# Small parameters loaded first, input-projection units 4 and 5 ahead of 6 and 7, products of 32 and 64 rows grouped, and new orders in both mixing stages of a two-layer hybrid encoder

## The chip, the cores and the metric

The kernel runs on one core of a Trainium2 chip. The metric is the device time in microseconds (us) of one execution. TensorE is PE in the rows (PEld is its weight load), VectorE is DVE, ScalarE is ACT, GpSimd is POOL and SyncE is SP. Every number is float32.

## What is computed

Two layers over 256 tokens of width 1024. Each layer has a token mixer of four head groups of 256 columns (retention, S5, Hyena, mLSTM) between one input and one output projection, then a channel mixer: dense SwiGLU in layer 0, the two best of eight experts in layer 1.

```python
h = layer_norm(x, ln_in_w, ln_in_b)
for l in range(DEPTH):                                  # DEPTH = 2
    proj = h @ w_in[l]                                  # 256 x 1024 @ 1024 x 3088
    y = concatenate([retention_mixer(p_ret, ...), s5_mixer(p_s5, ...),
                     hyena_mixer(p_hy, ...), mlstm_mixer(p_ml, ...)])
    h = layer_norm(DN_ALPHA * h + y @ w_out[l], ln1_w[l], ln1_b[l])
    f = swiglu(h, ...) if l % 2 == 0 else moe_swiglu(h, ...)
    h = layer_norm(DN_ALPHA * h + f, ln2_w[l], ln2_b[l])

# hyena_filters: a filter generator, one per layer
h = sin(fr * (z @ w1 + b1)); h = sin(fr * (h @ w2 + b2)); h = (h @ w3).reshape(L, 2, 2, D_GROUP)
h = h * exp(-t * rates)
return h * rsqrt(sum(square(h), axis=(0, 2)))
```

S5 is a diagonal complex recurrence, forward and backward in time. Hyena multiplies spectra twice: its value goes to frequencies, is multiplied by the filter's spectrum and comes back, and this is done for each of two filters. Retention and mLSTM are chunked attentions with decays, each followed by a norm over heads.

## The kernel before, in words

**How it is ordered.** No compiler orders the work. Each engine runs a list of calls written out by hand (`mix_0` and `mix_1` exist once for TensorE, once for ScalarE and once for VectorE), and the engines meet in named semaphores. An engine never passes a call that waits. So the place of a call in its list decides what is queued behind its wait.

**The input projection.** It is cut into 12 units. Units 0 to 5 give transposed outputs of 256 columns each (0 is the S5 input, 1 to 3 are Hyena's three parts, 4 and 5 are mLSTM's query and key), in two halves of eight products each, `unit(l, i, 0)` and `unit(l, i, 1)`. Units 6 and 7 are the retention's query and key for the two token tiles, 8 and 9 its value and gate, 10 and 11 mLSTM's value and gate. `UNITS` is the order, `UNIT_BANK` the PSUM bank of each, and `WIN_LOADS` says which units share one of the 2 MB weight loads into the three buffers `win0` to `win2`. Before a unit writes to its bank, the unit that had the bank must have been taken out: by `conv` on VectorE for units 1 to 5 (after ScalarE's `take_unit`), by `rotary` for 6 and 7, by `take_unit` for the others.

**S5.** Eight tiles. `s5_in` multiplies 32 rows of the input (K = 32) into a bank. VectorE then does for each tile `s5_tile_products`, `s5_tile_scan` and `s5_tile_rotate`, and GpSimd adds two halves (`b_sum`). `s5_y` gathers four tiles, `s5_skip` and `s5_glu` end it. The tables of sines that the tiles need come from steps `pre(l, 13)` to `pre(l, 20)`: VectorE reduces an angle, ScalarE takes sine and cosine. `s5_angle`, `pre(l, 11)` and `pre(l, 12)` prepare the coefficients.

**Hyena's filters.** Steps `pre(l, 0)` and `pre(l, 1)` are the two sine layers, `pre(l, 2)` to `pre(l, 5)` the third product with K = 64, window and square, `pre(l, 6)` the norm (a sum of squares by a product with ones, which two-column outputs take), `pre(l, 7)` to `pre(l, 10)` the filter's spectrum. In layer 0 these steps run inside `mix_0`, in layer 1 inside the dense channel mixer. `pre_norm` is VectorE's reciprocal of the norm.

**The rest of a mixing stage.** `hyena_transposes`, `hyena_forward`, `hyena_product` (VectorE), `hyena_inverse` and `hyena_gate` (VectorE), twice; `ret_transposes`, `ret_scores`, `ret_decay`, `ret_out` and `ret_norm`; `ml_gate_rows`, `ml_rows_a`, `ml_log`, `ml_rows_b`, `ml_columns`, `ml_cols`; `ml_rows_out` and `ml_rows_back` store the row maxima to memory and read them back spread over all partitions, both issued by ScalarE, the second after the first has landed; then for four heads `ml_mask`, `ml_exps`, `ml_weights`, `ml_out`, and last `ml_norm`, `head_scale(1)`, `head_out(1)`. The output projection is cut into 16 `out_product` calls, which fill TensorE's time between these; six of them stand behind `head_out(1)`.

**Loads.** SyncE issues all of them in one list. At the start: x, the first norm's weights, the identity, the first unit weights, all parameters of layer 0 (`pr`, 1728 KB), the positions and other small constants, and so on. A buffer of unit weights is loaded again when the last unit that reads it has been computed.

Of the kernel before, what the change touches and what calls it, by code (L numbers as in the profile page):

```python
# [19 lines left out]
P = 128  # L20
D = 1024
L = 256
# [45 lines left out]
def columns(sizes):  # L68
# [15 lines left out]
    ("s5_c", 2 * 16 * 32), ("s5_b", 512), ("glu", 512), ("hy_w3", 1024), ("hy_w12", 64), ("gate_w", KT * 16),  # L84
# [4 lines left out]
def trunk(nc, x, ln, const, par, w_in, w_out, ffn, moe, tab, out):  # L89
    ctx = ExitStack()  # L90
    with ctx:
# [82 lines left out]
        w1_feat = pr[64:97, PAR["hy_w12"][0]:PAR["hy_w12"][1]]  # L174
# [46 lines left out]
        fx_ = [[a[0:64, i * 256:(i + 1) * 256] for i in range(4)] for a in work]  # L221
# [3 lines left out]
        ct_s = [yTf[:, i * 512:(i + 1) * 512].rearrange("p (j c) -> p j c", c=32) for i in range(4)]  # L225
# [39 lines left out]
        s_pos = sem("positions_in")  # L265
        win_in = [sem(f"win{i}_loaded") for i in range(3)]
        loaded = [sem(f"ffn_slot{i}_loaded") for i in range(SLOTS)]
        freed = sem("ffn_chunk_split")
        up_in = [sem(f"ex_up_loaded{i}") for i in range(SLOTS)]
# [73 lines left out]

        def win_use(l, j):
# [18 lines left out]

        PRE1 = {u: k for u, k in enumerate(tuple(range(11, 21)) + tuple(range(7)), start=2)}
# [8 lines left out]
        def _(sp):  # L373
            def load_ff(i):
                s, _ = ff_use(i)
                if i >= 3:
                    sp.wait_ge(freed, i - 2)
                sp.dma_start(ring[s][:, :], ffn[i]).then_inc(loaded[s], 16)

            def load_win(l, j):  # L380
                b, _ = win_use(l, j)
                if j >= 3:
                    before = WIN_LOADS[{3: 1, 4: 2, 5: 0}[j]] if j < 6 else WIN_LOADS[j - 3]
# [16 lines left out]
            def load_ln(n):  # L400
                if n == 2:
                    sp.wait_ge(f_pm, 2)
                    sp.wait_ge(f_sq, 4)
# [5 lines left out]

            for t in range(TT):  # L410
# [117 lines left out]
        def _(pe):  # L528
# [41 lines left out]
            def pre(l, k):  # L570
# [6 lines left out]
                elif k == 1:  # L577
                    pe.wait_ge(f_sin, 2 * l + 1)
                    mm(pb[1][0:64, 0:L], W("hy_w12", 64), fx[3], start=True, stop=True).then_inc(f_mm, 1)
                elif k < 6:  # L580
                    j = k - 2
                    if j == 0:
                        pe.wait_ge(f_sin, 2 * l + 2)
                        pe.wait_ge(f_red, 2 * l + 2)
                    if j >= 2:
                        pe.wait_ge(f_win, 4 * l + j - 1)
                    mm(pb[j % 2][:, :], fx[3][:, (j // 2) * P:(j // 2 + 1) * P],
                       W("hy_w3", 64)[:, (j % 2) * 512:(j % 2 + 1) * 512], start=True, stop=True).then_inc(f_raw, 1)
                elif k == 6:
                    if l:  # L590
                        pe.wait_ge(f_sq, 5)
                        terms = [(0, 0)]
                    else:
                        pe.wait_ge(f_win, 4)
                        pe.wait_ge(f_sq, 2)
                        terms = [(t, d) for t in range(TT) for d in range(2)]
                    for j in range(4):
                        o, c = j // 2, j % 2
                        for i, (t, d) in enumerate(terms):
                            ins = mm(pb[0][:, 2 * j:2 * j + 2], fsq[t][:, o, d, c * P:(c + 1) * P], K("ones")[:, 0:2],  # L600
                                     start=(i == 0), stop=(i == len(terms) - 1))
# [14 lines left out]
            def unit(l, i, half):  # L616
# [6 lines left out]
                if half == 0:  # L623
# [3 lines left out]
                    elif p > 1:  # L627
                        pe.wait_ge(z_pr, 2 * l + 2)
# [155 lines left out]
            def s5_in(l, i):  # L784

                if i == 0:
                    pe.wait_ge(s_par, 16 * (l + 1))
                    pe.wait_ge(u_ev, l + 1)
                else:
                    pe.wait_ge(b_p, 8 * l + i)  # L790
                r = 32 * (i % 4)
# [32 lines left out]
            def out_product(l, group, b):  # L824
# [11 lines left out]
                if n == 0:  # L836
# [3 lines left out]
                    elif b == 2:  # L840
                        bank_evacuated(pe, l, 11)
# [10 lines left out]
            def mix_0():  # L852
                pe.wait_ge(ht_ready, 4)
                unit(0, 0, 0)
                unit(0, 0, 1)
                pre(0, 0)
                s5_in(0, 0)
# [4 lines left out]
                s5_in(0, 1)  # L862
                unit(0, 10, 0)
                unit(0, 10, 1)
                unit(0, 11, 0)
                unit(0, 11, 1)
                unit(0, 1, 0)
                s5_in(0, 2)
                unit(0, 1, 1)
                pre(0, 1)  # L870
                s5_in(0, 3)
                unit(0, 2, 0)
                unit(0, 2, 1)
                unit(0, 3, 0)
                unit(0, 3, 1)
                pre(0, 2)
                pre(0, 3)
                ml_gate_rows(0, 0)
                s5_in(0, 4)
                pre(0, 4)  # L880
                unit(0, 6, 0)
                pre(0, 5)
                unit(0, 6, 1)
                s5_y(0, 0)
                s5_in(0, 5)
                ml_gate_rows(0, 1)
                pre(0, 6)
                unit(0, 7, 0)
                pre(0, 7)
                pre(0, 8)  # L890
                unit(0, 7, 1)
                pre(0, 9)
                pre(0, 10)
                ml_columns(0)
# [1678 lines left out]
```

## Time and profile before

| what | value |
|---|---|
| time, median of 3 runs | 1611.61 us (1609.13 to 1612.51) |
| the profiled execution's own time | 1607.81 us |
| its span | 1606.0 us |
| mean granted TensorE clock | 0.990 of full |
| TensorE matmul busy | 1562.5 us, 97% |
| VectorE busy | 1337.2 us, 83% |
| ScalarE busy | 963.7 us, 60% |
| GpSimd busy | 47.1 us, 3% |

All times in the rows are counted from the start of the span. The stages lie in it so: first norm to 15.6 us, mixing stage of layer 0 to 214, dense channel mixer to 425.7, mixing stage of layer 1 to 591, router and experts to the end. A float32 matmul stands as two records in the rows, so x16 are eight products. Busy times of a stretch do not add up to a bound by themselves: what ends a stretch is read from the waits in it.

### The profile page before, as it was taken

The numbers are of one execution on the slowest core, as the hardware profiler recorded it, in microseconds if no ns is written. First come the engines' busy times: TensorE is split into PE (matmuls) and PEld (weight loads), VectorE is DVE, ScalarE is ACT, GpSimd is POOL, SyncE is SP. The second block draws the span as 40 slices with busy tenths as digits, with TensorE's granted clock in tenths as the row PEclk, the third lists the DMA queues.
The fourth block names the chain that finished last, engine by engine and source line by source line (L and its number), as shares of the span: only waits on it lengthen the run. The fifth ranks groups of instructions, "written<-read, shape, count | busy, mean of one in ns | idle before, by whom it ended". The sixth has DMA issues, their size and how long they took to land.

```text
span 1606.0 us, 18396 instructions
## 1 busy us (share of the span) xinstructions
PE 1562.5 (97%) x7492; PEld 1235.9 (77%) x7492; DVE 1337.2 (83%) x1435; ACT 963.7 (60%) x1000; POOL 47.1 (3%) x34
## 2 busy tenths in 40 slices
PE   7998999999999899999999999999999999999997
PEld 5656679988766667888888888888888788888885
DVE  6999567766498867889989998988998989898897
ACT  3321455644212346777777677677777777777775
POOL 0112000000021100000000000000000000000000
PEclk9998999999999999999999999999999999999999
DMA  8231445644424156999889999989899989999981
GB/s 334 105 133 52 157 159 231 245 174 171 193 105 142 61 230 274 372 369 379 342 341 370 355 369 371 354 333 372 345 378 373 348 343 368 380 361 373 365 338 52
DMA packets 41676, 446.33 MB, mean 278 GB/s; under 512 B 4457, under 2 KB 4585, under 8 KB 8433
## 3 DMA queue, kind: packets, MB, share of 16 engines
q1 hardware_dynamic: 39360, 438.78, 70.2%
q10 hardware_dynamic: 2224, 6.31, 1.1%
q8 instruction: 61, 1.00, 0.2%
q14 instruction: 31, 0.25, 0.0%
HBM read 439.81 MB, written 5.26 MB: 277 GB/s over the span
## 4 chain that ended last, share of the span: by engine, by line
PE 80%; DVE 13%; ACT 4%; issue 1%; DMA 1%; POOL 0%; SPq 0%; DVEq 0%; ACTq 0%
PE bank L1145 35%; PE bank L1172 16%; PE bank L1030 8%; PE bank L640 4%; PE bank L1040 4%; PE bank L648 3%; PE bank L846 3%; DVE ring_lo L2198 2%; PE bank L1153 1%; DVE ring_lo L2340 1%; ACT ex_up_hi L1498 1%; PE bank L1093 1%; DMA pr<-par 1%; PE bank L1116 1%; ACT ex_w_hi L1624 1%
## 5 line engine op out<-in xcount | busy, mean ns | idle before, releaser
L2198 DVE TENSOR_TENSOR ring_lo<-ring,ex_up_hi 128x2048 fp32r<-128x2048 f32 x224 | 512.9, 2290 | 51.3 <-ACT ex_up_hi L1498 49.8
L1498 ACT ACTIVATE ex_up_hi<-ring 128x2048 fp32r<-128x2048 f32 x224 | 429.2, 1916 | 105.9 <-PE bank L1145 105.9
L1145 PE MATMUL bank<-ex_up_hi,ex_x_hi 128*128 128x512 f32 x896 | 362.6, 405 | 5.6 <-DVE ring_lo L2198 4.7
L1145 PE MATMUL bank<-ring_lo,ex_x_hi 128*128 128x512 f32 x896 | 350.7, 391 | 0.0
L1145 PE MATMUL bank<-ex_up_hi,ex_x_lo 128*128 128x512 f32 x896 | 349.7, 390 | 0.0
L2340 DVE TENSOR_TENSOR ring_lo<-ring,ex_w_hi 128x2048 fp32r<-128x2048 f32 x111 | 253.2, 2281 | 0.0
L1624 ACT ACTIVATE ex_w_hi<-ring 128x2048 fp32r<-128x2048 f32 x111 | 211.5, 1905 | 0.0
L1145 PEld LDWEIGHTS bank<-ex_up_hi,ex_x_hi 128*128 128x128 f32 x896 | 168.3, 188 | 43.8 <-DVE ring_lo L2198 12.3
L1145 PEld LDWEIGHTS bank<-ring_lo,ex_x_hi 128*128 128x128 f32 x896 | 168.2, 188 | 36.7
L1145 PEld LDWEIGHTS bank<-ex_up_hi,ex_x_lo 128*128 128x128 f32 x896 | 168.8, 188 | 30.5
L1172 PE MATMUL bank<-ex_w_hi,ex_mid_hi 128*128 128x512 f32 x448 | 174.5, 389 | 0.0
L1172 PE MATMUL bank<-ring_lo,ex_mid_hi 128*128 128x512 f32 x448 | 174.3, 389 | 0.0
L1172 PE MATMUL bank<-ex_w_hi,ex_mid_lo 128*128 128x512 f32 x448 | 174.3, 389 | 0.0
L1172 PEld LDWEIGHTS bank<-ex_w_hi,ex_mid_hi 128*128 128x128 f32 x448 | 84.1, 188 | 17.7 <-DVE ring_lo L2340 0.3
L1172 PEld LDWEIGHTS bank<-ring_lo,ex_mid_hi 128*128 128x128 f32 x448 | 84.1, 188 | 17.5
L1172 PEld LDWEIGHTS bank<-ex_w_hi,ex_mid_lo 128*128 128x128 f32 x448 | 84.1, 188 | 17.4
L1030 PE MATMUL bank<-ff_x_hi,ff_up_hi 128*128 128x256 f32 x336 | 96.1, 286 | 0.0
L1030 PE MATMUL bank<-ff_x_hi,ff_up_lo 128*128 128x256 f32 x336 | 95.1, 283 | 0.0
L1030 PE MATMUL bank<-ff_x_lo,ff_up_hi 128*128 128x256 f32 x336 | 95.1, 283 | 0.0
L1618 ACT ACTIVATE sc<-bank 128x256 f32<-128x256 f32 x112 | 43.0, 384 | 84.2 <-PE bank L1145 84.2
L648 PE MATMUL bank<-win,hT 128*128 128x512 f32 x192 | 93.4, 619 | 0.0
L640 PE MATMUL bank<-hT,win 128*128 128x256 f32 x384 | 85.4, 381 | 3.1 <-ACT hT L1247 1.6
(355 smaller groups left out, 2028.1 us busy)
## 6 DMA issues: line engine op xcount, KB each, us to landing
ring<-moe SPq DMA_DIRECT2D x112, 2048.0 KB, 7.6
ring<-moe SPq DMA_DIRECT2D x112, 1024.0 KB, 7.4
ring<-ffn SPq DMA_DIRECT2D x11, 3072.0 KB, 11.1
win<-w_in SPq DMA_DIRECT2D x12, 2048.0 KB, 8.6
win<-w_out SPq DMA_DIRECT2D x4, 2048.0 KB, 10.2
lnb<-ln SPq DMA_DIRECT2D x4, 1024.0 KB, 5.7
tab<-yT ACTq DMA_DIRECT2D x8, 512.0 KB, 5.5
pr<-par SPq DMA_DIRECT2D x2, 1728.0 KB, 11.1
```

Source lines behind the costliest of these rows:

```text
L640: ins = mm(b[:, half * L:(half + 1) * L], w[:, k, c:c + P], hT[:, k, :], start=(k == 0), stop=(k == KT - 1))
L648: ins = mm(b[:, :], x, w[:, k, :], start=(k == 0), stop=(k == KT - 1))
L846: ins = mm(bank[b][:, :], yT[:, k, t * P:(t + 1) * P], w[:, k, :], start=(n == 0 and i == 0), stop=(n == 3 and i == 1))
L1030: ins = mm(bank[4 + u % 2][:, w * L:(w + 1) * L], (ff_up if u else ff_up_first)[j][:, w, k, :], ff_x[i][:, k, :], start=(k == 0 and n == 0 ...
L1040: ins = mm(bank[2 * t + hf][:, :], ff_mid[i][:, u % 2, t * P:(t + 1) * P], w2[j][:, hf * 512:(hf + 1) * 512], start=False, stop=(u == NU - ...
L1145: ins = mm(b[:, :], ex_x[x % 3][x_][:, k, :], (ex_up_hi, lo)[w_][:, k, :], start=(k == 0 and m == 0), stop=(k == KT - 1 and m == 2))
L1172: ins = mm(bank[2 * (x % 2) + hf][:, :], ex_mid[a][:, g % 2, f * P:(f + 1) * P], w2[b], start=(c == 0 and f == 0 and m == 0), stop=(c == N ...
L1498: act(ex_up_hi[:, HS * q:HS * (q + 1), :], wt[:, HS * q:HS * (q + 1), :], ACT.Copy).then_inc(e_uh, 1)
L1618: act(sil[g % 2], bank[4 + g % 2][:, 0:L], ACT.Silu).then_inc(e_sil, 1)
L1624: act(ex_w2_hi[g % 2][:, :], ring[here][:, UPW:SLOT], ACT.Copy).then_inc(e_wh, 1)
L2198: tt(ring_lo[s][:, half], ring[s][:, half], hi.bitcast(F32), ALU.subtract).then_inc(e_ul, 1)
L2340: tt(ring_lo[s][:, UPW:SLOT], ring[s][:, UPW:SLOT], ex_w2_hi[g % 2][:, :].bitcast(F32), ALU.subtract).then_inc(e_wl, 1)
```

## The change

Names of lines are those of the kernel before in the text, of each kernel in its rows. The change has five parts.

1. **Loads at the start.** The last 128 columns of the parameters come first by themselves (`s_small`), the positions come ahead of the first unit weights, the other parameters behind them. `s5_step`, `s5_angle` and ScalarE's `pre(0, 11)` move ahead of the first norm.
2. **Units.** 4 and 5 are computed ahead of 6 and 7, all in banks 5 and 6, and the weight loads are paired anew.
3. **Row groups.** `s5_in` takes several tiles at once, in different banks and row groups (two and two in layer 0, four in layer 1). The third filter product puts its two halves of K = 64 on rows 0 to 63 and 64 to 127.
4. **The norm of layer 0's filters.** VectorE adds up the squares first (`square_total(0)`), as it did in layer 1, and TensorE multiplies 4 times by ones instead of 16 times.
5. **Orders.** `mix_0` and `mix_1` of TensorE, ScalarE and VectorE are written in another order.

```diff
-UNITS = (0, 8, 9, 10, 11, 1, 2, 3, 6, 7, 4, 5)
+UNITS = (0, 8, 9, 10, 11, 1, 2, 3, 4, 5, 6, 7)
-UNIT_BANK = (5, 6, 5, 6, 5, 6, 5, 6, 5, 6, 1, 2)
+UNIT_BANK = (5, 6) * 6
-WIN_LOADS = ((0, (0, 3)), (1, (8, 9)), (2, (10, 11)), (1, (1, 2)), (2, (6, 7)), (0, (4, 5)))
+WIN_LOADS = ((0, (0, 1)), (1, (8, 9)), (2, (10, 11)), (1, (2, 3)), (0, (4, 5)), (2, (6, 7)))
...
+        def s5_bank(l, i):
+            if l:
+                return i if i < 4 else 3
+            return 2 + i % 2 if i < 4 else 3
...
+            few = PAR["gate_b"][0]
+            sp.dma_start(pr[:, few:PAR_W], par[0, :, few:PAR_W]).then_inc(s_small, 16)
             for t in range(TT):
                 sp.dma_start(h[:, t, :], x[t * P:(t + 1) * P, :]).then_inc(s_x[t], 16)
             load_ln(0)
             first = slice(*CONST["ident"])
             sp.dma_start(cst[:, first], const[:, first]).then_inc(s_id, 16)
+            sp.dma_start(cst[:, first.stop:CONST_W], const[:, first.stop:CONST_W]).then_inc(s_pos, 16)
             load_win(0, 0)
-            sp.dma_start(pr[:, :], par[0]).then_inc(s_par, 16)
-            sp.dma_start(cst[:, first.stop:CONST_W], const[:, first.stop:CONST_W]).then_inc(s_pos, 16)
+            sp.dma_start(pr[:, 0:few], par[0, :, 0:few]).then_inc(s_par, 16)
...
+                    for o in range(2):
+                        r = slice(64 * o, 64 * o + 64)
+                        mm(pb[o][:, :], fx[3][r, t * P:(t + 1) * P], W("hy_w3")[r, 0:512],
+                           start=True, stop=True).then_inc(f_raw, 1)
...
-            def s5_in(l, i):
+            def s5_in(l, first, n):
...
+                    pe.wait_ge(b_p, 8 * l + first)
                 for s in range(2):
-                    ins = mm(bank[3][:, s * L:(s + 1) * L], s5b[r:r + 32, i // 4, s, :],
-                             uT[r:r + 32, i // 4, :], start=True, stop=True)
-                ins.then_inc(b_mm, 1)
+                    for i in range(first, first + n):
+                        r = 32 * (i % 4)
+                        ins = mm(bank[s5_bank(l, i)][:, s * L:(s + 1) * L], s5b[r:r + 32, i // 4, s, :],
+                                 uT[r:r + 32, i // 4, :], start=True, stop=True)
+                        if s:
+                            ins.then_inc(b_mm, 1)
...
-            def square_total():
-
-                fsq = fsq_[1]
-                ve.wait_ge(f_sq, 4)
+            def square_total(l):
+
+                fsq = fsq_[l]
+                ve.wait_ge(f_sq, 3 * l + 2)
                 link(tt(fsq[0], fsq[0], fsq[1], ALU.add))
                 tt(fsq[0][:, :, 0, :], fsq[0][:, :, 0, :], fsq[0][:, :, 1, :], ALU.add).then_inc(f_sq, 1)
```

Three places of the orders. **VectorE at the start of the program.** Before, the last part of the first norm (h), then `s5_angle` on `pr` and `small`, then `pre(0, 11)`:

```order
L1674 SCALAR_TENSOR_TENSOR h<-h,small,lnb 128x1024
L1748 TENSOR_TENSOR small<-pr,small 128x16
L1749 TENSOR_TENSOR small<-pr,small 128x16
L1750 TENSOR_SCALAR small<-small 128x16
L1751 TENSOR_SCALAR small<-small 128x16
L1752 TENSOR_TENSOR small<-small 128x16
L1785 TENSOR_TENSOR small<-small 128x16
```

Of the change, the same `s5_angle` and then the norm's statistics:

```order
L1758 TENSOR_TENSOR small<-pr,small 128x16
L1759 TENSOR_TENSOR small<-pr,small 128x16
L1760 TENSOR_SCALAR small<-small 128x16
L1761 TENSOR_SCALAR small<-small 128x16
L1762 TENSOR_TENSOR small<-small 128x16
L1663 BN_STATS small<-h 128x6 x2
```

The five operations on the S5 angle now stand ahead of the norm; `pre(0, 11)` still stands behind it, and `pre(0, 12)` has gone behind `pre(0, 16)`.

**TensorE in the middle of layer 0's mixing stage.** Before, unit 3 (the first L640 row), the four products of `pre(0, 2)` to `pre(0, 5)` (L587) with halves of unit 6 (L648) between them, `s5_y(0, 0)` (L807); the 16 products with ones (L600) are the next row:

```order
L640 MATMUL bank6<-hT,win0_66 128x256 x16
L587 MATMUL bank0<-pr,sc 128x512
L587 MATMUL bank1<-pr,sc 128x512
L736 MATMUL bank4<-cst,small 4x128 x4
L793 MATMUL bank3<-uT,pr 128x256 x2
L587 MATMUL bank0<-pr,sc 128x512
L648 MATMUL bank5<-win2_68,hT 128x512 x4
L587 MATMUL bank1<-pr,sc 128x512
L648 MATMUL bank5<-win2_68,hT 128x512 x4
L807 MATMUL bank7<-ring3,pr 32x256 x16
L793 MATMUL bank3<-uT,pr 128x256 x2
L736 MATMUL bank4<-cst,small 4x128 x4
```

Of the change, from unit 3 (first row) to the row ahead of the first spectrum product, with the products with ones as L610:

```order
L648 MATMUL bank6<-hT,win1_67 128x256 x16
L648 MATMUL bank5<-hT,win0_66 128x256 x8
L604 MATMUL bank0<-pr,sc 128x512
L604 MATMUL bank1<-pr,sc 128x512
L802 MATMUL bank3<-uT,pr 128x256 x2
L648 MATMUL bank5<-hT,win0_66 128x256 x8
L648 MATMUL bank6<-hT,win0_66 128x256 x8
L817 MATMUL bank7<-ring3,pr 32x256 x16
L744 MATMUL bank4<-cst,small 4x128 x4
L610 MATMUL bank0<-cst,spec 128x2 x4
L648 MATMUL bank6<-hT,win0_66 128x256 x8
L744 MATMUL bank4<-cst,small 4x128 x4
```

Four halves of units 4 and 5 (`win0_66`, banks 5 and 6) now stand here; before they stood behind the second `s5_y`, as the two L640 rows of this piece show:

```order
L807 MATMUL bank7<-ring2,pr 32x256 x2
L640 MATMUL bank1<-hT,win0_66 128x256 x16
L640 MATMUL bank2<-hT,win0_66 128x256 x16
L678 MATMUL bank0<-cst,yT 128x256 x8
L688 MATMUL bank4<-cst,sc 128x128 x4
```

The L678 row there is `hyena_inverse(0, 1)`, which in the change follows `s5_y(0, 1)` at once.

**TensorE at the start of layer 1's mixing stage.** Inside unit 8, before, one S5 tile (L793):

```order
L648 MATMUL bank6<-win1_67,hT 128x512
L793 MATMUL bank3<-uT,pr 128x256 x2
L647 MATMUL bank4<-pr,hT 128x16
L648 MATMUL bank6<-win1_67,hT 128x512
L647 MATMUL bank4<-pr,hT 128x16
```

Of the change, four tiles in four banks:

```order
L656 MATMUL bank6<-win1_67,hT 128x512
L802 MATMUL bank0<-uT,pr 128x256
L802 MATMUL bank1<-uT,pr 128x256
L802 MATMUL bank2<-uT,pr 128x256
L802 MATMUL bank3<-uT,pr 128x256
L802 MATMUL bank0<-uT,pr 128x256
L802 MATMUL bank1<-uT,pr 128x256
L802 MATMUL bank2<-uT,pr 128x256
L802 MATMUL bank3<-uT,pr 128x256
L655 MATMUL bank4<-pr,hT 128x16
```

Tiles 1, 2 and 3 stood alone between later units before.

## Rows read from the trace of the kernel before

**Rows 1.** Busy times by stretch: us, width, engines, PEclk, DMA share, GB/s.

```profile
15.60:105.40 89.80, 88.15 (x350) 55.62 (x351) 81.10 (x147) 33.37 (x57) 9.42 (x4) 0.97 0.45 180
105.40:134.20 28.80, 25.95 (x83) 14.32 (x81) 28.35 (x42) 7.47 (x13) 4.71 (x2) 0.86 0.33 110
134.20:193.00 58.80, 54.84 (x286) 41.87 (x285) 38.81 (x80) 22.73 (x45) 6.38 (x3) 0.94 0.20 75
193.00:214.00 21.00, 19.82 (x52) 8.90 (x52) 14.78 (x32) 4.06 (x8) 1.65 (x1) 1.00 0.56 227
214.00:425.70 211.70, 209.92 (x1408) 187.14 (x1406) 140.63 (x213) 117.61 (x165) 1.20 (x4) 1.00 0.52 197
425.70:591.00 165.30, 159.76 (x697) 105.26 (x698) 125.89 (x212) 40.40 (x75) 22.21 (x10) 0.99 0.35 131
```

**Rows 2.** The chain that ended last, its start: start us, us, what.

```profile
3.38 14.19 DMA pr<-par
```

**Rows 3.** DMA issues in 3.3 to 4.3 us: count, size, us to landing.

```profile
cst<-const SPq DMA_DIRECT2D x1, 640.0 KB, 15.3
```

**Rows 4.** VectorE in order of time, layer 0: start us, us, line, operation.

```profile
12.43 1.28 DVE L1674 SCALAR_TENSOR_TENSOR h<-h,small,lnb 128x1024 f32<-128x1024 f32 x1
20.94 0.18 DVE L1785 TENSOR_TENSOR small<-small 128x16 f32<-128x16 f32 x1 [2.11 <-ACT small L1283]
69.57 0.86 DVE L1837 SCALAR_TENSOR_TENSOR cv<-bank,pr,cv 128x255 f32<-128x255 f32 x2
104.12 1.23 DVE L2041 TENSOR_TENSOR ring<-ring 128x1024 f32<-128x1024 f32 x1
```

**Rows 5.** The order of time behind the first S5 rotation.

```profile
46.47 2.81 DVE L1822 TENSOR_SCALAR yT<-cst,small 128x256 f32<-128x256 f32 x2
46.51 2.35 POOL L521 TENSOR_TENSOR ring<-ring 128x1024 f32<-128x1024 f32 x1 [37.87 <-DVE ring L2041]
```

**Rows 6.** TensorE in order of time at full clock.

```profile
90.63 1.12 PE L587 MATMUL bank<-pr,sc 64*128 64x512 f32 x2
109.03 3.60 PE L612 MATMUL bank<-sc,cst 128*128 128x512 f32 x8
496.02 3.72 PE L669 MATMUL bank<-sc,cst 128*128 128x256 f32 x16
499.58 7.03 PE L648 MATMUL bank<-win,hT 128*128 128x512 f32 x16
523.54 1.12 PE L793 MATMUL bank<-uT,pr 32*128 32x256 f32 x4
524.59 1.13 PE L713 MATMUL bank<-ret 64*128 64x256 f32 x8
```

**Rows 7.** TensorE around the products with ones, layer 0.

```profile
98.71 5.26 PE L600 MATMUL bank<-cst,spec 128*128 128x2 f32 x32
103.83 5.37 PE L648 MATMUL bank<-win,hT 128*128 128x512 f32 x8
```

**Rows 8.** Busy times by stretch, where the granted clock fell.

```profile
100.00:107.00 7.00, 7.00 (x25) 5.32 (x26) 6.86 (x10) 2.25 (x3) 1.58 (x1) 0.53 0.00 1
126.00:140.00 14.00, 11.70 (x41) 8.78 (x41) 13.83 (x23) 1.20 (x2) 2.57 (x2) 0.63 0.20 62
144.00:149.00 5.00, 4.31 (x14) 3.42 (x13) 4.90 (x9) 2.67 (x4) 0.00 (x0) 0.66 0.00 0
550.00:562.00 12.00, 8.51 (x34) 5.32 (x35) 8.61 (x20) 8.86 (x17) 1.66 (x1) 0.86 0.18 60
```

**Rows 9.** Units 4 and 5 of layer 0, and VectorE's wait for them.

```profile
154.93 14.08 PE L640 MATMUL bank<-hT,win 128*128 128x256 f32 x64 [0.52 <-DVE yT L1883]
163.20 0.87 DVE L1837 SCALAR_TENSOR_TENSOR cv<-bank,pr,cv 128x255 f32<-128x255 f32 x2 [4.36 <-ACT cv L1311]
```

**Rows 10.** ScalarE's queue: the row maxima out and back, layer 0.

```profile
119.54 0.52 ACTq L1362 DMA_DIRECT2D tab<-ring  x1
124.06 0.41 ACTq L1367 DMA_DIRECT2D ring<-tab  x1
```

More of the change, by code:

```diff
@@ L220, in trunk @@
         pm_ = [a[:, 0:2048].rearrange("p (s t o c) -> p s t o c", s=2, t=TT, o=2) for a in work]
-        fx_ = [[a[0:64, i * 256:(i + 1) * 256] for i in range(4)] for a in work]
+        fx_ = [[a[:, i * 256:(i + 1) * 256] for i in range(4)] for a in work]
         tab_work = [yTf, cvf]
@@ L342, in ff_use, with up_use @@
             return FF_SLOTS[i % 3], 16 * (i // 3 + 1)
+        def up_use(g):
+            of_ffn = sum(ff_use(i)[0] == MOE_SLOTS[g % SLOTS] for i in range(NC_FF))
+            return 16 * (of_ffn + g // SLOTS + 1)
         def win_use(l, j):
@@ L382, in load_win @@
                 if j >= 3:
-                    before = WIN_LOADS[{3: 1, 4: 2, 5: 0}[j]] if j < 6 else WIN_LOADS[j - 3]
+                    before = WIN_LOADS[{3: 1, 4: 0, 5: 2, 6: 3, 7: 5}[j]]
                     sp.wait_ge(pj, 12 * l + POS[before[1][1]] + 1)
@@ L963, in mix_1 @@
                 unit(1, 3, 1)
-                ml_gate_rows(1, 0)
-                s5_y(1, 0)
+                unit(1, 4, 0)
                 hyena_transposes(1, 0)
-                ml_gate_rows(1, 1)
-                s5_in(1, 5)
+                s5_in(1, 6, 1)
                 hyena_forward(1, 0)
+                unit(1, 5, 0)
+                unit(1, 4, 1)
+                unit(1, 5, 1)
+                hyena_inverse(1, 0)
+                unit(1, 7, 0)
+                s5_in(1, 7, 1)
+                ml_columns(1)
                 unit(1, 6, 0)
+                hyena_transposes(1, 1)
                 unit(1, 6, 1)
-                hyena_inverse(1, 0)
-                ml_columns(1)
-                s5_in(1, 6)
-                hyena_transposes(1, 1)
-                unit(1, 7, 0)
                 unit(1, 7, 1)
@@ L1430, in mix_0 @@
                 pre(0, 10)
-                ml_rows_out(0)
+                ml_log(0)
                 hyena(0, 0)
-                ml_rows_back(0)
                 ret_qk(0)
                 hyena(0, 1)
+                silu_qk(0, 5)
+                ml_rows_out(0)
+                ml_rows_back(0)
+                ml_floor(0)
                 s5_gelu(0)
-                take_unit(0, 4)
-                silu_qk(0, 4)
-                take_unit(0, 5)
-                silu_qk(0, 5)
-                ml_floor(0)
+                s5_gate(0)
                 head_out(0, 4, W("ret_gn"), 0)
                 ml_exps(0, 0)
-                s5_gate(0)
                 ml_exps(0, 1)
@@ L1512, in ff_w2_hi @@
                 act(dst[0][:, :], w2, ACT.Copy).then_inc(d_wh, 1)
+            s5_step(0)
+            s5_radius(0)
+            pre(0, 11)
             evacuate_h(0)
@@ L1745, in s5_angle @@
                 dt_, x1, th, tf = s5v[0:4]
-                ve.wait_ge(s_par, 16 * (l + 1))
+                if l:
+                    ve.wait_ge(s_par, 32)
+                else:
+                    ve.wait_ge(s_small, 16)
                 ve.wait_ge(c_dt, l + 1)
@@ L2117, in mix_0 @@
                 s5_skip(0)
-                conv(0, 4)
+                hyena_gate(0, 1)
                 head_scale(0)
-                conv(0, 5)
-                hyena_gate(0, 1)
+                s5_end(0)
                 ml_mask(0, 0)
                 ml_mask(0, 1)
-                s5_end(0)
+                ml_mask(0, 2)
                 ml_weights(0, 0)
                 ml_weights(0, 1)
-                ml_mask(0, 2)
+                ml_mask(0, 3)
                 ml_weights(0, 2)
-                ml_mask(0, 3)
                 ml_weights(0, 3)
```

364 lines of the change are left out of this document (177 added, 187 removed).

## The prediction

> **What bounds the kernel now.** I first asked in which stretches the change can act. The busy times by stretch [rows 1] show two kinds. In the dense channel mixer TensorE works 209.92 of 211.70 us: a microsecond of matmul less is a microsecond less there. In the two mixing stages neither engine is full. The reader is to see the second to fourth row: from 134.2 to 193 us VectorE works 38.81 of 58.80 us and TensorE 54.84, and the chain goes to and fro between them. Router and experts hold none of the edited steps; they only start earlier.
>
> Then the start. The chain begins with the parameters' load, 14.19 us [rows 2]. VectorE is done with the first norm at 12.43 + 1.28 = 13.7 us and its `pre(0, 11)` starts at 20.94 [rows 4]. Third, who waits inside layer 0's stage: units 4 and 5 take TensorE 14.08 us, and VectorE waits 4.36 us for the first of them [rows 9], because they stand behind the second `s5_y` and nothing else is left to do. Fourth, the clock: it fell in four places [rows 8].
>
> **The change, part by part.** I lay the new lists side by side and cut layer 0's stage into four stretches.
>
> *First stretch, to `pre_norm`: VectorE sets it.* Before, VectorE needs 105.4 - 20.9 = 84.5 us from `pre(0, 11)` on, working nearly without a break [rows 1, 4]. Now the small parameters come first, so `pre(0, 11)` follows the norm. One more issue ahead of x costs about 0.4 us (0.41 to 0.52 for one issue) [rows 10], so it starts at 14.2. The positions, which it needs too, landed 15.3 us after their issue [rows 3]; they now stand ahead of the 2 MB of weights and the parameters, with some 2.8 MB ahead of and in them, about half of what lay ahead before, so by 10 to 11 us. The first unit's weights get 0.7 MB more ahead of them, some 1.6 us, which I take to be hidden by the norm; uncovered they would cost up to 1.6 us. Same work: 14.2 + 84.5 = 98.7. New in it: `conv(0, 4)`, two groups of 0.86, 1.75 us [rows 4]; `square_total(0)`, an operation like the 1.23 us one and one of half the size, 1.9 us. And one hold more: a TENSOR_SCALAR behind a rotation took 2.81 us while GpSimd added for 2.35 [rows 5], against an estimated 0.6 us for its like, so 2.2 us. There were two such followers before this point (`pre(0, 19)` and `pre(0, 0)`); now there are three (`pre(0, 18)`, `pre(0, 0)`, `pre(0, 20)`). Sum 104.5. The norm then passes TensorE and ScalarE, estimated at 1.4 us from a quarter of the 5.26 us of the 16 products [rows 7]: 105.9, where `pre_norm` stood at 105.4. TensorE's place in this stretch: it waits three times for VectorE or ScalarE (before unit 10, before `pre(0, 1)`, before `pre(0, 4)`), by my laying-out 2.5, 2.1 and 2.7 us. It has room for that.
>
> *Second stretch, to `hyena_inverse(0, 0)`: TensorE sets it.* Half of unit 5 (3.5) and the gate rows (0.5) bring it to about 109.6. Then four spectrum products, 7.2; one S5 tile, 1.1; transposes, 0.7; unit 6, 7.0; `hyena_forward`, 3.7; unit 7, 7.0 [rows 6]: 136, against 134.2 before. VectorE has its product ready at 135. So up to here the change loses 1.8 us, though it has put two units into the stretch.
>
> *Third stretch, to the last `ml_out`.* Before 58.8 us [rows 1]. Units 4 and 5 leave it: 14.1, all on the chain [rows 9]. One of the two `conv` calls was on the chain too: 1.7. Left 43.0. Laid out call by call I get 43.2 and the same order of waits: VectorE sets it from `hyena_gate` to the first masks, then ScalarE's exponentials.
>
> *Fourth stretch.* From the last `ml_out` to the last output product it was 21.0 us [rows 1]. It keeps the same norm and the same six products behind `head_out(1)`: 21.0. Layer 0's stage ends at 136 + 43 + 21 = 200 where it ended at 214: **-14.0 us**.
>
> *Dense mixer.* Four filter products of K = 64, 1.12 us each [rows 6], become two pairs. The row of the retention's scores shows what a pair costs: four products over 64 rows and 256 columns, 1.13 us, as long as the two over 32 rows in the S5 row (1.12). So a pair costs one: 2 x about 1.0 less, **-1.9 us**.
>
> *Layer 1's stage.* TensorE works 159.8 of 165.3 us [rows 1]. Tiles 0 to 3 cost four times about 1.1 us and now once, if four row groups run side by side: -3.3. Of 5.5 us idle, the new order leaves 1.7 by my laying-out, since units 4 and 5 fill the waits for the Hyena steps: -3.8. VectorE is due within a microsecond of TensorE at several places: +1.0. **-6.1 us**.
>
> No row shows four row groups. The bounds are 1.1 us (side by side) and 4.5 (one after another); the nearest row is the pair, which costs exactly one, so I take 1.1 and keep 3.3 us for the range. The Trainium skill, TensorEngine Tiling (Array Packing), Theoretical Speedup, gives up to 4 times for contractions of at most 32 rows; by it the four cost 1.1 us, by the other bound 4.5, and the sum changes by 3.3 us.
>
> *The clock.* The granted clock cost 7.0 x 0.47 + 14.0 x 0.37 + 5.0 x 0.34 + 12.0 x 0.14 = 11.9 us of TensorE [rows 8], at the lower of its two levels, 1.2 GHz, for most of each stretch. The unit half behind the products with ones took 5.37 us instead of 3.5 [rows 6, 7]. Those 16 products are gone, but new waits come (2.5, 2.1, 2.7 us, and about 1 us twice in the third stretch). My sum is at 2.4 GHz throughout. Between no loss (0) and as much as before (11.9) I take half: **+6.0**.
>
> *Holds.* `square_total(0)`, `ml_rows_a(0)` and `rotary(1, 6)` now stand within 2.35 us of a rotation, part of it covered: **+1.1**.
>
> Sum: -14.0 - 1.9 - 6.1 + 6.0 + 1.1 = -14.9. Against the profiled execution's own 1607.8 us (span 1606.0 and 1.8 around it) that is 1592.9. That execution was 3.8 us below the median of the runs, 1611.6; from the median it is 1596.7, which is my number.
>
> **The rivals.**
>
> *Smaller gain: the row groups of 32 do not run side by side, or the clock takes as much as before.* For it: the new waits on TensorE. Against: the pair row. Four groups in a row give 3.3 back; a clock loss of 11.9 gives 5.9 more: 1600 to 1606.
>
> *Taken back by the row maxima.* `ml_rows_out` moves behind `hyena(0, 1)` and `silu_qk(0, 5)` on ScalarE, to about 149 us, and `ml_rows_back` can issue 4.5 us later (119.54 to 124.06) [rows 10]. Behind this wait on ScalarE's list stand `ml_floor`, `s5_gelu` and `s5_gate`, and VectorE's `ml_mask` waits for the landing at about 165. A landing at 159 to 160 is hidden; from 165 on each microsecond costs one, and with 180 the whole of layer 0's gain is gone: 1611. Against: memory is quiet there in the same stretch (DMA share 0.20) [rows 1].
>
> *The other side: TensorE at half clock in the second stretch.* It is now TensorE's, 26 us of products, and ahead of it the 2.7 us wait and 10 us of small pieces. If the clock falls at 93 us and stays down to 136, some 36 us of work double: +36 against the 20.9 us that the sum gives without any clock loss, so 1611.6 - 20.9 + 36 = 1627. It decides from 20.9 us lost. Against: before, the longest such fall lasted under 14 us [rows 8], and units 6 and 7 keep the array dense. The Trainium skill, TensorE: Matmul & The Clock Gate, HAM oscillation, says that gaps between bursts throttle the clock again and again; by that rule the waits that the change puts on TensorE cost more than their length, which is this rival. The trace agrees that a gap does it: the 126 to 140 us row.
>
> **How the numbers follow.** As forecast, 1590 to 1601: 0.60. Smaller gain, 1601 to 1607: 0.22. Larger than 22 us: 0.05. Taken back or hidden anyway, within 3.2 us (0.2%, about what a measurement of this kernel tells from no change): 0.07. Slower: 0.06. The range takes the first two: 1589.5 (no clock loss, no holds) to 1606.5. Faster 0.87, same 0.07, slower 0.06.
>
> **What would show it.** In the changed kernel's trace: the first angle step at 16 instead of 27 us; `pre_norm` near 106; the first inverse near 136; the last `ml_out` near 179; the end of layer 0's stage near 200. The four S5 tiles of layer 1 in 1.1 us. Layer 1's stage 159 us long. TensorE waits of over 2 us only ahead of `pre(0, 1)`, unit 10 and `pre(0, 4)`. I would be wrong if TensorE were late at `hyena_inverse(0, 0)` by more than 5 us, if `ml_mask(0, 0)` waited for the spread maxima, or if the granted clock stood low through a whole stretch.

## The result and the profile after

| what | before | changed |
|---|---|---|
| time, median of 4 runs | 1610.37 us (1607.46 to 1612.51) | 1586.65 us (1583.90 to 1587.69) |
| the profiled execution's own time | 1607.81 us | 1586.18 us |
| its span | 1606.0 us | 1584.4 us |
| mean granted TensorE clock | 0.990 | 0.995 |

The ratio is 0.9849, with an interval of 0.9836 to 0.9862: 1.5% faster, 23.7 us by the medians and 21.6 us by the two spans. The forecast was 1596.7, its range began at 1589.5; the gain is larger than both. (The median of before was 1611.6 when the forecast was made, from three of these four runs.)

Busy times by stretch, cut where the same work ends as in [rows 1] (to `pre_norm`, to the first inverse, to the last `ml_out`, to the last output product, dense mixer, layer 1's mixing stage):

```profile
15.60:107.70 92.10, 85.89 (x361) 56.92 (x359) 86.60 (x145) 33.01 (x56) 11.78 (x5) 0.96 0.45 179
107.70:137.10 29.40, 29.40 (x93) 15.95 (x91) 28.81 (x43) 9.38 (x15) 4.72 (x2) 1.00 0.00 1
137.10:180.80 43.70, 39.38 (x246) 28.71 (x246) 35.17 (x75) 21.07 (x42) 4.01 (x2) 1.00 0.45 155
180.80:201.75 20.95, 20.95 (x54) 9.37 (x53) 14.79 (x32) 4.07 (x8) 1.65 (x1) 1.00 0.65 264
201.75:411.30 209.55, 207.72 (x1410) 187.06 (x1408) 140.71 (x213) 117.75 (x165) 1.20 (x4) 1.00 0.52 200
411.30:571.60 160.30, 158.76 (x706) 104.39 (x707) 131.58 (x220) 41.65 (x78) 22.22 (x10) 1.00 0.35 134
```

Layer 0's stage ends at 201.75 instead of 214.0: 12.25 us. The dense mixer gives 211.70 - 209.55 = 2.15. (The border of 214.0 is rounded up: the instruction that starts at 201.75 starts at 213.8 in the kernel before, so 0.2 us of the first gain belong to the second.) For layer 1 the two rows of before that matter are the last output products and the first product of the experts (the border of 591 in [rows 1] lies 3.4 us ahead of the stage's real end):

```profile
585.67 8.75 PE L846 MATMUL bank<-win,yT 128*128 128x512 f32 x20
...
611.21 0.47 PE L1145 MATMUL bank<-ex_up_hi,ex_x_hi 128*128 128x512 f32 x1 [0.74 <-DVE ex_x_lo L2322]
```

So the stage took 594.4 - 425.7 = 168.7 us and takes 160.3: 8.4 us. The router between took 611.2 - 594.4 = 16.8 us, and now 589.6 - 571.6 = 18.0: 1.2 us lost. The experts take 994.8 us in both. Sum: 12.25 + 2.15 + 8.4 - 1.2 = 21.6.

TensorE in order of time, after. The first and third rows answer to waits that the prediction laid out (before `pre(0, 1)` and `pre(0, 4)`). The second, unit 11, ran at a low clock:

```profile
56.05 0.70 PE L592 MATMUL bank<-sc,pr 64*128 64x256 f32 x2 [2.19 <-ACT sc L1272]
...
57.74 8.83 PE L656 MATMUL bank<-win,hT 128*128 128x512 f32 x16
...
94.36 1.13 PE L604 MATMUL bank<-pr,sc 64*128 64x512 f32 x4 [1.30 <-DVE yT L1784]
...
137.08 3.72 PE L686 MATMUL bank<-cst,yT 128*128 128x256 f32 x16
...
422.73 1.15 PE L802 MATMUL bank<-uT,pr 32*128 32x256 f32 x16
...
589.62 0.47 PE L1148 MATMUL bank<-ex_up_hi,ex_x_hi 128*128 128x512 f32 x1 [0.75 <-DVE ex_x_lo L2336]
```

Unit 11 takes 8.83 us where its like takes 7.03 [rows 6]. The last row but one is the four S5 tiles, in 1.15 us. Windows (us, TensorE's busy time, PEclk, DMA share, GB/s) show that layer 0's falls of before [rows 8] are gone (layer 1's too: its stage stands at 1.00 in the table above). New falls came: at unit 11, in the router, and one at 27 to 31 us (0.79 in 25 to 33 us):

```profile
57.00:63.00 6.00, 6.00 (x17) 0.72 0.00 0
100.00:107.00 7.00, 6.69 (x59) 1.00 0.00 1
126.00:140.00 14.00, 14.00 (x48) 1.00 0.15 35
573.00:583.00 10.00, 9.79 (x74) 0.83 0.92 393
```

VectorE and ScalarE's queue in order of time, after: the norm's end, `pre(0, 11)`, the hold behind a rotation, `square_total(0)`, `pre_norm`, the row maxima out and back, and the mask that needs them:

```profile
13.83 1.28 DVE L1681 SCALAR_TENSOR_TENSOR h<-h,small,lnb 128x1024 f32<-128x1024 f32 x1
15.04 0.17 DVE L1796 TENSOR_TENSOR small<-small 128x16 f32<-128x16 f32 x1
...
38.80 2.80 DVE L1834 TENSOR_SCALAR yT<-cst,small 128x256 f32<-128x256 f32 x2
...
103.78 1.80 DVE L1742 TENSOR_TENSOR spec<-spec 128x1024 f32<-128x1024 f32 x1
105.61 0.69 DVE L1743 TENSOR_TENSOR spec<-spec 128x512 f32<-128x512 f32 x1
107.66 0.18 DVE L1749 RECIPROCAL small<-small 128x4 f32<-128x4 f32 x1 [1.35 <-ACT small L1279]
...
146.47 0.52 ACTq L1369 DMA_DIRECT2D tab<-ring  x1
147.91 0.40 ACTq L1374 DMA_DIRECT2D ring<-tab  x1
...
166.35 1.43 DVE L1970 SCALAR_TENSOR_TENSOR cv<-ring,cst 128x256 f32<-128x256 f32 x4
```

The mask has no wait behind it in its row: the maxima had landed (the DMA engines fell quiet at about 153 us).

### The profile page after: what moved, and what is told of

Same layout as the page of the kernel before. It is cut to its first block, busy times and chain, and to the rows that moved or that the text cites. A ratio compares the mean times of both kernels' runs of the same rounds, so it can differ in the third digit from the quotient of the medians.

```text
span 1584.4 us, 18355 instructions
## 1 busy us (share of the span) xinstructions
PE 1543.7 (97%) x7468; PEld 1225.3 (77%) x7468; DVE 1342.3 (85%) x1437; ACT 964.6 (61%) x1001; POOL 47.1 (3%) x34
## 3 DMA queue, kind: packets, MB, share of 16 engines
HBM read 439.81 MB, written 5.26 MB: 281 GB/s over the span
## 4 chain that ended last, share of the span: by engine, by line
PE 79%; DVE 15%; ACT 4%; issue 1%; DMA 0%; SPq 0%; DVEq 0%
PE bank L1148 36%; PE bank L1175 16%; PE bank L1033 8%; PE bank L1043 4%; PE bank L856 4%; PE bank L656 2%; DVE ring_lo L2211 2%; PE bank L1156 1%; DVE ring_lo L2354 1%; PE bank L648 1%; ACT ex_up_hi L1502 1%; PE bank L1096 1%; PE bank L1119 1%; ACT ex_w_hi L1631 1%; DVE ring L2053 1%
## 5 line engine op out<-in xcount | busy, mean ns | idle before, releaser
L2348 DVE TENSOR_TENSOR ex_mid_lo<-bank,ex_mid_hi 128x256 fp32r<-128x256 f32 x112 | 47.5, 424 | 48.2 <-ACT ex_mid_hi L1593 48.2
```

Of the source, the lines that this page charges most:

```text
L2348: tt(ex_mid[1][:, g % 2, :], bank[4 + g % 2][:, 0:L], ex_mid[0][:, g % 2, :].bitcast(F32), ALU.subtract).then_inc(e_mid, 1)
```

## The experiments

The marks used below are the first inverse of layer 0, the end of layer 0's stage, the length of layer 1's stage and the first expert product. In the changed kernel they are 137.1, 201.75, 160.3 and 589.6 us.

**The start.** First the changed kernel with its start undone:

```diff
-            sp.dma_start(pr[:, few:PAR_W], par[0, :, few:PAR_W]).then_inc(s_small, 16)
...
-            sp.dma_start(cst[:, first.stop:CONST_W], const[:, first.stop:CONST_W]).then_inc(s_pos, 16)
             load_win(0, 0)
-            sp.dma_start(pr[:, 0:few], par[0, :, 0:few]).then_inc(s_par, 16)
+            sp.dma_start(pr[:, :], par[0]).then_inc(s_par, 16)
+            sp.dma_start(cst[:, first.stop:CONST_W], const[:, first.stop:CONST_W]).then_inc(s_pos, 16)
...
```

Not shown are the lines that put `s5_step`, `s5_angle` and `pre(0, 11)` behind the norm again.

> The changed kernel with only the start put back: parameters in one load behind the first unit weights, s5_angle and pre(0, 11) behind the norm. Theory (VectorE sets the first stretch): its first table step falls from 17.1 to some 23 or later, everything to pre_norm moves by the same 6 us, and TensorE's waits grow: 1592 to 1595. Rival (TensorE sets the stretch too): its waits of 4.2 us in all take most of it and the time is 1587 to 1589.

Then the kernel before with the new start alone:

> The kernel before with only the new start: small parameters and positions first, s5_angle and pre(0, 11) ahead, pre(0, 12) behind pre(0, 16). Theory A (VectorE alone sets the first stretch, as the prediction had it): 6 to 8 us less, 1603 to 1605. Theory B (TensorE is as full, 88.15 of 89.80 us): at most its waits of 1.4 us, 1608 to 1610, and the gain of the start comes only where work of TensorE is taken away too.

The undone start gave 1595.01 us, ratio 0.9918 (0.9890 to 0.9945) against 0.9849. Its four runs spread from 1590.99 to 1599.17, two at a mean clock of 0.992 and two at 0.988; the profiled one is the fastest, so its trace is the better measure of the edit. VectorE in order of time, start undone:

```profile
20.95 0.18 DVE L1795 TENSOR_TENSOR small<-small 128x16 f32<-128x16 f32 x1 [2.11 <-ACT small L1289]
...
114.61 0.18 DVE L1748 RECIPROCAL small<-small 128x4 f32<-128x4 f32 x1 [1.72 <-ACT small L1278]
```

`pre(0, 11)` is 5.9 us later than in the changed kernel, `pre_norm` 6.95, the stage's end 6.9 (208.7). VectorE sets this stretch in the changed kernel, as the prediction had it. Alone in the kernel before, the same edit gave 1605.95 us by the median of ten runs, between the ranges of the two theories, and a ratio of 0.9986 (0.9973 to 1.0000), about 2 us. The trace speaks for theory B:

```profile
104.47 0.18 DVE L1752 RECIPROCAL small<-small 128x4 f32<-128x4 f32 x1
...
127.40 1.14 PE L706 MATMUL bank<-cst,lnb 128*128 128x128 f32 x8 [4.39 <-DVE small L1963]
```

`pre_norm` moves by 0.9 us only, for TensorE is as full there (88.07 of 88.90 us). And what TensorE gains goes into a longer wait at `ret_transposes`, 4.39 against 2.75 us. Layer 0's stage ended at 213.0, 0.8 us earlier. The other 1.4 us of this execution came in layer 1 (167.3 us instead of 168.7), where the start changes nothing and the clock did not fall. So the same edit is worth 7 us in one order and about 1 in the other.

Last, the small parameters' load issued by ScalarE:

```diff
-            sp.dma_start(pr[:, few:PAR_W], par[0, :, few:PAR_W]).then_inc(s_small, 16)
...
+            ac.dma_start(pr[:, few:PAR_W], par[0, :, few:PAR_W]).then_inc(s_small, 16)
             s5_step(0)
```

> The changed kernel with the small parameters' load issued by ScalarE instead of SyncE. In the changed kernel it stands ahead of x on SyncE's list and the first norm ends at 15.1 us against 13.7 before, 1.4 us later. Theory (VectorE sets the first stretch, so the norm's 1.4 us lie on the path): the norm ends 0.5 to 1.4 us earlier and pre_norm, the first inverse and the end of the stage move with it: 1585.3 to 1586.2. Rival: no change in the marks past 60 us.

Time 1584.93 us, ratio 0.9843 (0.9827 to 0.9858). The marks do not move against the changed kernel's second run set (further below): `pre_norm` 107.16 against 107.24, stage's end 201.2 against 201.3. The rival is the likelier, but half a microsecond could not be told here: with the load on SyncE's list the norm ended anywhere from 14.2 to 15.1 us in the changed kernel's and its variants' profiled executions, and at 14.65 in this one. The lower time goes with the router's clock, which did not fall in the profiled execution: 16.4 us instead of 18.0.

**The norm.** The changed kernel with 16 products with ones again, and the kernel before with `square_total(0)` and 4 (the lines are of the first):

```diff
-                    pe.wait_ge(f_sq, 3 * l + 3)
+                        pe.wait_ge(f_win, 4)
+                        pe.wait_ge(f_sq, 2)
+                        terms = [(t, d) for t in range(TT) for d in range(2)]
...
-                square_total(0)
                 pre_norm(0)
```

> The changed kernel with only the norm of layer 0's filters put back: VectorE's square_total(0) is gone and TensorE multiplies 16 times by ones. Theory (the small pieces bring the clock down): 3.9 us more of products on TensorE, which sets the end of this stretch, and a low granted clock behind them as before (0.53 in 100 to 107 us), some 5 us more: 1594 to 1597 against 1586.7. Rival (only waits of TensorE bring it down): the clock stays at 1.00 from 100 to 115 us and the time is 1590 to 1591.

> The kernel before with only the norm of layer 0's filters changed: square_total(0) on VectorE, 4 products instead of 16. VectorE gets 2.5 us more, TensorE 3.9 us less, so pre_norm moves about 2 us earlier. Theory (small pieces bring the clock down): the row of 100 to 107 us shows 1.00 instead of 0.53 and the half unit behind is 1.8 us shorter: 1605 to 1607. Rival: clock as before and 1608 to 1609. The low clock of 126 to 140 us follows a wait of 2.75 us and stays by both.

With the 16 products back: 1591.29 us, ratio 0.9884 (0.9865 to 0.9904). TensorE in order of time, then the window:

```profile
106.82 4.59 PE L617 MATMUL bank<-cst,spec 128*128 128x2 f32 x32
111.27 6.08 PE L655 MATMUL bank<-hT,win 128*128 128x256 f32 x16
```

```profile
110.00:116.00 6.00, 6.00 (x18) 5.10 (x19) 4.24 (x6) 0.65 (x2) 0.00 (x0) 0.50 0.00 0
```

Behind the two-column products the clock is at 1.2 GHz, as in [rows 7]: the half unit takes 6.08 instead of 3.70 us. The inverse comes at 143.3, 6.2 us later, of which 3.5 are the products (4.59 against 1.05) and 2.4 the clock. Layer 0's stage ended 7.3 us later (209.0), and 1.6 came back in the router, whose clock did not fall in this execution. The mechanism of the theory is there, about half the size that it had; the time, 1591.3, is below its 1594 and just above the rival's bound.

The same edit in the kernel before made it slower: 1613.14 us, ratio 1.0022 (1.0012 to 1.0031), against both theories. TensorE in order of time:

```profile
111.05 1.87 PE L593 MATMUL bank<-cst,spec 128*128 128x2 f32 x8 [10.53 <-DVE spec L1729]
112.78 5.98 PE L641 MATMUL bank<-win,hT 128*128 128x512 f32 x8
```

I had counted the products and not their new wait. The 16 products stood at 98.7 us and needed only ScalarE; the 4 need VectorE's sum, which stands behind the rotation (104 us in the kernel before, 106 here), and TensorE waits 10.53 us. The second operation of the sum took 2.71 us beside GpSimd's addition, where it takes 0.69 otherwise. The changed kernel puts units there: its wait is 0.31.

**The clock.** The changed kernel with one more wait, and with the same wait filled:

```diff
+                keep_busy(12, 2)         # only in the second of the two
+                pe.wait_ge(b_p, 7)
                 hyena_transposes(0, 0)
```

> The changed kernel with one added wait: TensorE waits for VectorE's products of S5 tile 6 ahead of hyena_transposes(0, 0), at 119 us, where it had no wait, about 2.9 us. Nothing of VectorE's is waiting for it there. Theory (a gap of this length brings the clock down and the loss lies on the path): 2.9 us and some 5 us of half clock behind it, 1593 to 1596 against 1586.7, with a low granted clock from 122 us on. Rival (the dense units around it keep the clock up): 2.9 us alone, 1589 to 1590.

> As the one with the added wait at 119 us, but 12 transposing-size products of the identity into a free bank run on TensorE ahead of the wait, about 3 us, so that the gap is filled. Nothing is computed with them. Theory (the gap costs more than its length by way of the clock): 1589.7, faster than the unfilled gap by 3 to 6 us. Rival: the same time as the unfilled gap.

The wait alone: 1588.92 us, ratio 0.9855 (0.9839 to 0.9872); filled: 1588.93, the same ratio. By time the rival holds. The trace of the unfilled one still shows the clock:

```profile
122.83 0.76 PE L669 MATMUL bank<-cst,cv 128*128 128x128 f32 x4 [2.91 <-DVE ring L2023]
123.39 8.66 PE L656 MATMUL bank<-win,hT 128*128 128x512 f32 x16
```

The unit behind the wait takes 8.66 us and not 7.03. So a wait of 2.9 us ahead of full units costs 1.6 us more than its length, a third of the 5 expected. The stage ended 4.7 us later (206.5). The span rose by 3.0 only, for the router took 16.4 us here and 18.0 in the changed kernel's own profiled executions. Filled, this unit took 7.03; in that execution the clock fell at 145 to 155 us (0.83) and in the router instead, and the end was the same. The medians can therefore not tell what filling the wait is worth.

The kernel before, its 2.75 us wait at 125 us filled:

> The kernel before with 11 products of the identity, 2.75 us, into a free part of a bank on TensorE ahead of ret_transposes(0), where it waits 2.75 us for VectorE at 125 us. Nothing is computed with them. Theory (the low clock of 126 to 140 us comes from this wait, and its 5.2 us lie on the path): the row from 126 to 140 us shows a clock near 1.00 and the time is 4 to 5 us less, 1605 to 1607. Rival (that part waits for VectorE anyway, so the clock costs nothing there): 1609 to 1612, whatever the clock does.

Time 1609.58 us, ratio 1.0001 (0.9990 to 1.0012): the rival. The filling was not complete, 1.92 us of wait were left behind it, and the clock of 126 to 140 us rose to 0.88 from 0.63, not to 1.00. The inverse came 1.3 us earlier (132.9), the stage's end not (214.5). The next row of TensorE shows where it went:

```profile
144.23 0.65 PE L661 MATMUL bank<-cst,cv 128*128 128x128 f32 x4 [3.75 <-DVE cv L1894]
```

This wait was 0.81 us before. VectorE, busy 13.83 of the 14 us from 126 on [rows 8], set the end of that stretch.

**Row groups.** The changed kernel with the four S5 tiles of layer 1 one at a time in one bank, and with the loops exchanged:

```diff
-                return i if i < 4 else 3
+                return 3
...
-                s5_in(1, 0, 4)
+                s5_in(1, 0, 1)
                 unit(1, 8, 1)
+                s5_in(1, 1, 1)
```

> The changed kernel with the first four S5 tiles of layer 1 one at a time again, in one bank, between the units. Theory (four row groups run side by side, 1.1 us in all): 3.3 us slower, 1590. Rival (they cost the same either way, or VectorE sets the stretch): within 1 us of 1586.7.

```diff
-                for s in range(2):
-                    for i in range(first, first + n):
+                for i in range(first, first + n):
+                    for s in range(2):
```

> The changed kernel with the loops of s5_in exchanged: both halves of a tile right behind each other, then the next tile, so that neighbours in the list use the same rows of the array. Banks and places are unchanged. Theory A (products run side by side only where the next one in the list has other rows): the four tiles take 2 to 2.5 us instead of 1.15, time up by 1 to 2 us. Theory B (the array takes them as they fit): 1.15 us and no change.

Medians 1587.34 (ratio 0.9849, 0.9833 to 0.9865) and 1586.00 (0.9841, 0.9825 to 0.9857): neither differs from the changed kernel by more than the runs do. By time the rival of the first holds. The length of the stage, which the router's clock does not touch, tells them apart. Busy times of that stage, tiles alone, then loops exchanged:

```profile
410.58:574.40 163.82, 162.48 (x706) 106.05 (x707) 131.30 (x220) 41.59 (x78) 22.18 (x10) 1.00 0.35 132
```

```profile
411.33:571.60 160.27, 158.79 (x706) 104.43 (x707) 131.46 (x220) 41.59 (x78) 22.18 (x10) 1.00 0.35 134
```

And the four tiles with the loops exchanged, in order of time:

```profile
422.76 1.17 PE L802 MATMUL bank<-uT,pr 32*128 32x256 f32 x16
```

163.8 against 160.3: 3.5 us, where 3.3 was forecast. The total hides half of it: in the profiled execution with the tiles alone the router took 16.4 us and not 18.0. With neighbours on the same rows the four tiles take 1.17 us: theory B, the order of the loops does not matter here.

**Three parts without the orders.** The kernel before with the new start, the paired filter products and the four tiles at once, and its old lists:

> The kernel before with the new start, the paired filter products and four S5 tiles at once in layer 1, but with the old order of units and of both mixing stages and the 16 products with ones. By the terms of the sum: start, at most 2.2 us as the run with the start alone gave; dense mixer 1.9; S5 tiles 3.3; in all 7.4, 1603. Theory (these parts add up and the orders carry the rest, some 17 us): 1602 to 1605. Rival (the parts give more together than alone, the orders less): below 1599.

Time 1607.88 us, ratio 0.9986 (0.9973 to 0.9998), about 2 us: not the 7.4 of the sum, and the opposite of its rival. The dense mixer gave its 2 us (209.55 us long). Layer 0's stage ended at 215.9, 2.1 us later than before, with a wait of 3.82 us for VectorE at 145 us. Layer 1's stage took 167.3 us, as long as in the run with the new start alone, though TensorE had 3.3 us less to do. The clock accounts for some of it: it stood at 0.92 and 0.74 in two 5 us windows from 465 on, 1.7 us. These parts together gave about a tenth of the whole gain; the rest came with the units, the norm and the new orders.

**The changed kernel again:**

> The changed kernel once more, in five rounds, as the measure for the other variants. If the granted clock falls at varying places from run to run, its runs spread over 4 us or more and the mean clock goes with the time; if the clock's falls belong to the places of the program, the spread stays below 2 us.

Time 1586.12 us (1585.31 to 1587.56), mean clocks 0.994 and 0.995: a spread of 2.3 us, between the two marks that I had set. The kernel before, timed 49 times beside the variants, spread over 1605.94 to 1614.22, and its time goes with the mean clock of the run (correlation -0.88):

```
clock   0.992   0.991   0.990   0.989   0.988   0.987
runs    4       5       10      19      7       4
median  1606.3  1608.5  1609.9  1610.8  1611.9  1613.3
```

## Why the prediction was wrong

The direction, the mechanisms and most places were as forecast; the size was not: 14.9 us against 21.6 between the profiled executions, and 10 us between the forecast and the measured time. **The step that failed is "The clock", +6.0.** I took half of the loss of before because the new waits on TensorE (2.5, 2.1, 2.7 us) looked like the old ones. They do bring the clock down, but it cost 1.2 us of the path, all in the router, where no fall was expected. Of the 6.7 us between the sum and the gain of the profiled execution this term is 4.8; layer 1's stage gave 2.3 more than forecast, the holds' 1.1 and the dense mixer's 0.25 come on top, and layer 0's stage took back 1.75. In layer 0 it cost nothing in the profiled execution: both of its falls lie ahead of 65 us, in the stretch that VectorE sets.

The run with exchanged loops shows this best, its list for layer 0 being the same. TensorE in order of time, then the window:

```profile
56.79 7.13 PE L656 MATMUL bank<-win,hT 128*128 128x512 f32 x16
...
93.38 1.13 PE L604 MATMUL bank<-pr,sc 64*128 64x512 f32 x4 [2.72 <-DVE yT L1784]
```

```profile
95.00:100.00 5.00, 5.00 (x16) 3.90 (x15) 4.93 (x9) 0.00 (x0) 0.00 (x0) 0.66 0.00 0
```

Here unit 11 ran at full clock, the wait ahead of `pre(0, 4)` was 2.72 us instead of 1.30, and the clock fell behind that one. VectorE in order of time, exchanged loops: the norm's last part, the taking out of `pre(0, 4)`'s products, and `conv(0, 4)`; then the taking out in the changed kernel:

```profile
12.90 1.28 DVE L1681 SCALAR_TENSOR_TENSOR h<-h,small,lnb 128x1024 f32<-128x1024 f32 x1
...
94.54 1.29 DVE L1784 TENSOR_TENSOR yT<-bank,cst 128x512 f32<-128x512 f32 x2 [1.22 <-PE bank L604]
...
102.37 0.87 DVE L1849 SCALAR_TENSOR_TENSOR cv<-bank,pr,cv 128x255 f32<-128x255 f32 x2 [1.30 <-ACT cv L1318]
```

```profile
95.52 1.29 DVE L1784 TENSOR_TENSOR yT<-bank,cst 128x512 f32<-128x512 f32 x2 [1.22 <-PE bank L604]
```

From the end of the norm to this taking out VectorE needed 80.4 us in both executions (14.2 to 94.5 here, 15.1 to 95.5 in the changed kernel). So the changed kernel's falls at 27 to 31 us and at unit 11 took the place of waits and cost nothing. The fall behind the longer wait did cost: `conv(0, 4)` waited 1.30 us for its unit, and from the taking out to the first inverse it took 42.6 us against 41.6, 1.0 us more. The two executions come to the same mark (137.15 and 137.08) only because the norm ended 0.9 us earlier here.

Eight profiled executions share this list up to the products with ones. Four show the changed kernel's falls, and three the fall at 95 to 100 us, with the same wait of 1.3 us at `conv(0, 4)`. In the eighth (the filled wait) the fall at unit 11 was longer, 0.66 in 55 to 65 us, and the taking out came 1.2 us later after the norm.

**What put the time outside the range was a second step**, the one from the profiled execution to the median. I set the result 3.8 us above the profiled execution for both kernels. The changed kernel's profiled run lies 0.5 us under its median: 3.3 of the 10 us. The kernel before loses more to the clock in most runs than in the profiled one (the table), and that went too: 2 us beyond the 21.6. The range's low end, no clock loss and no holds, is a gain of 22.0; the 21.6 of the profiled executions lie just inside it, by 0.4, and the 3.3 us put the median 2.9 us outside. To a gain larger than 22 us I had given 0.05.

Step by step:
- *First stretch*: 105.9 forecast, 107.7 measured. Right that VectorE sets it (the undone start). Wrong that neither engine was full there before: TensorE worked 88.15 of 89.80 us [rows 1], which is why the start alone gave so little in the kernel before. Two sizes were off: the norm ended 1.4 us later than before in this execution (0.5 to 1.4 in all with the new start), not the 0.4 of one issue, and `square_total(0)` took 2.5, not 1.9. The hold was there, 2.80 us.
- *Second stretch*, TensorE's: 30 us forecast, 29.4 measured. *Third*: 43 and 43.7. *Fourth*: 21.0 and 20.95. The stage ended at 201.75, forecast 200 without the holds.
- *Holds*, +1.1: 0.6 of it is seen at `square_total(0)`, whose first operation took 1.80 us beside GpSimd's addition and 1.22 in the run with exchanged loops, where it came later. The rest was not separated.
- *Dense mixer*: 1.9 and 2.15.
- *Layer 1's stage*: 6.1 and 8.4. The four tiles were right (3.5 measured). Of the 2.3 us left, 1.4 to 1.7 is the fall of [rows 8] at 550 to 562 us, which I had not taken out of the base (the stage took 1.4 us less in the run of the kernel before with the start alone, where it did not fall); the waits that I had allowed for (1.0) did not come.

*The rivals*: the row groups run side by side, so the smaller gain did not come; the row maxima were read back at 148 us and hidden; TensorE at half clock through the second stretch did not happen (1.00 throughout), and the added wait of 2.9 us there cost 1.6 us beyond its length, not 36. The rule on gaps in the Trainium skill (TensorE: Matmul & The Clock Gate, HAM oscillation) is borne out in that waits bring the clock down; what a fall cost was 1.0 to 2.4 us, and nothing where TensorE waited next for longer than it had lost.

What stays open: why the clock falls behind a wait in one execution and not in the next of the same list, as in the router (fell in both profiled executions of the changed kernel, not in the one with exchanged loops) and at 95 to 100 us. How much of the 21.6 us the units' move gives by itself was not tried; by the trace it shortened the third stretch from 58.8 to 43.7 us.

## What to carry to other kernels

An edit's worth is that of the engine which sets the stretch, so the same part can be worth 7 us in one order and 1 in another, or cost time (the norm's sum alone, 10.53 us of wait): sum the parts only within one laid-out order. A clock loss is put on the path only where TensorE itself sets the end; where it waits for another engine next, the loss comes out of the wait, as far as no other engine waits for the slowed product in between. When the base itself loses time to the clock, take that loss out of the base before giving the range its low end, and do not carry the distance between the base's profiled run and its median over to the changed kernel.

## What the runs showed of the hardware

- Four S5 tiles, of two products over 32 rows each, in different row groups and banks take 1.15 us against 1.12 for one tile alone, and 1.17 when neighbours in the list use the same rows.
- Sixteen two-column products take 4.59 us (5.26 in the kernel before), and the full-width half unit behind them ran at 1.2 GHz in the profiled execution (6.08 against 3.70 us).
- The mean granted clock of a run explains most of the spread of the kernel before: 7 us between 0.992 and 0.987. The changed kernel, at 0.994 to 0.996, spreads over 3.8 us.
- The end of the first norm moves by itself: 13.7 to 14.5 us in the four profiled executions with the old start, 14.2 to 15.1 in the nine with a load of 64 KB issued ahead of x, 14.65 with that load on ScalarE's queue. So the load ahead of x costs it some 0.6 us by the means of these, and one pair of traces could show anything from nothing to 1.4.
- VectorE operations took longer beside GpSimd's addition (2.35 to 3.38 us): a TENSOR_SCALAR pair 2.80 us against 0.62, TENSOR_TENSOR operations 2.71 against 0.69 and 1.80 against 1.22.
